# Feed-forward weight pairs by seven products: operand combinations and third weight sums moved to GpSimd, the first pair's first sum to VectorE, the second step as a plain unit

## The reference

```python
def swiglu(x, w_in, w_out):
    gate, up = jnp.split(x @ w_in, 2, axis=-1)      # w_in: 1024 x 5632, w_out: 2816 x 1024
    return (jax.nn.silu(gate) * up) @ w_out

h = layer_norm(DN_ALPHA * h + 0.5 * swiglu(h, ffn_w_in[i, 0], ffn_w_out[i, 0]), ln_g[i, 0], ln_b[i, 0])
```

## Time and profile before

| | us |
|---|---|
| median of 3 runs (1524.52 to 1525.26) | 1524.89 |
| the profiled execution, its own time | 1523.43 |
| its span, first to last instruction | 1521.5 |
| PE busy | 1490.0 (98%) |
| DVE busy | 1112.7 (73%) |
| ACT busy | 833.1 (55%) |
| POOL busy | 156.4 (10%) |
| granted TensorE clock, mean | 0.994 |

### The profile page before, as it was taken

The page is one execution under the profiler, slowest core; times in us unless marked ns, Lnnn a source line. Parts: engine busy times, 40 slices in busy tenths (PEclk is TensorE's granted clock), DMA queues, the critical chain, the costliest instruction groups (busy, mean ns, idle before and its releaser), DMA issues.

```text
span 1521.5 us, 18598 instructions
## 1 busy us (share of the span) xinstructions
PE 1490.0 (98%) x7654; PEld 1258.1 (83%) x7654; DVE 1112.7 (73%) x1135; ACT 833.1 (55%) x839; POOL 156.4 (10%) x152
## 2 busy tenths in 40 slices
PE   8899999989999999999999989999999999999997
PEld 6688888878888788888888868888898888888886
DVE  5887687787877977787567787867686556785555
ACT  5656467565565665554434556555636566354443
POOL 0400020110002000024021200002002200020000
PEclk9999999999999999999999999999999999999999
DMA  9777454477837777555544677746444434465551
GB/s 356 268 231 229 182 204 169 150 262 277 295 106 296 218 241 256 166 227 188 179 160 169 224 249 226 269 163 237 154 167 142 164 139 166 166 222 194 193 191 58
DMA packets 46595, 310.08 MB, mean 204 GB/s; under 512 B 5568, under 2 KB 6016, under 8 KB 10800
## 3 DMA queue, kind: packets, MB, share of 16 engines
q1 hardware_dynamic: 38592, 270.35, 47.8%
q0 software_dynamic: 6112, 34.80, 9.9%
q10 hardware_dynamic: 1808, 3.74, 0.6%
HBM read 282.60 MB, written 1.05 MB: 186 GB/s over the span
## 4 chain that ended last, share of the span: by engine, by line
PE 83%; DVE 7%; DMA 6%; issue 1%; ACT 1%; POOL 1%; SPq 0%; POOLq 0%; DVEq 0%; ACTq 0%
PE psum L1988 16%; PE psum L1992 15%; PE psum L1991 15%; PE psum L2097 7%; PE psum L2124 6%; PE psum L2101 4%; DVE weights_lo L1174 4%; DMA weights_raw_more<-weights_raw_more 3%; PE psum L2240 3%; PE psum L2237 3%; PE psum L2236 3%; PE psum L2131 3%; DMA weights_raw_more<-in_weights 2%; PE psum L2020 1%; PE psum L2033 1%
## 5 line engine op out<-in xcount | busy, mean ns | idle before, releaser
L1174 DVE TENSOR_TENSOR weights_lo<-weights_raw,weights_hi 128x2048 fp32r<-128x2048 f32 x191 | 440.9, 2312 | 198.0 <-ACT weights_hi L609 196.6
L609 ACT ACTIVATE weights_hi<-weights_raw 128x2048 fp32r<-128x2048 f32 (+1 forms) x198 | 372.4, 1883 | 194.9 <-PE psum L1992 136.2
L1174 DVE TENSOR_TENSOR weights_lo<-weights_raw_more,weights_hi 128x2048 fp32r<-128x2048 f32 x56 | 128.2, 2289 | 70.5 <-ACT weights_hi L609 70.5
L1988 PE MATMUL psum<-weights_hi,hidden_hi 128*128 128x512 f32 x416 | 163.9, 394 | 3.3 <-DVE weights_lo L1174 3.3
L1991 PE MATMUL psum<-weights_lo,hidden_hi 128*128 128x512 f32 x416 | 162.4, 390 | 0.0
L1992 PE MATMUL psum<-weights_hi,hidden_lo 128*128 128x512 f32 x416 | 162.1, 390 | 0.0
L1988 PE MATMUL psum<-weights_hi,operand 128*128 128x512 f32 x384 | 151.5, 394 | 0.0
L1991 PE MATMUL psum<-weights_lo,operand 128*128 128x512 f32 x384 | 149.8, 390 | 0.0
L609 ACT ACTIVATE weights_hi<-weights_raw_more 128x2048 fp32r<-128x2048 f32 x56 | 107.1, 1913 | 70.1 <-DMA weights_raw_more<-weights_raw_more 39.2
L1992 PE MATMUL psum<-weights_hi,operand 128*128 128x512 f32 x352 | 137.2, 390 | 0.0
L2097 PE MATMUL psum<-operand,weights_hi 128*128 128x512 f32 x544 | 129.4, 390 | 0.0
(11 more groups left out here) (386 smaller groups left out, 2799.9 us busy)
## 6 DMA issues: line engine op xcount, KB each, us to landing
weights_raw<-in_weights SPq DMA_DIRECT2D x198, 1024.0 KB, 4.8
weights_raw_more<-in_weights SPq DMA_DIRECT2D x56, 1024.0 KB, 8.9
weights_raw_more<-weights_raw_more POOLq DMA_DIRECT2D x20, 1024.0 KB, 7.2
ln_rows<-in_ln_rows POOLq DMA_DIRECT2D x16, 512.0 KB, 7.3
weights_raw_more<-weights_raw POOLq DMA_DIRECT2D x4, 1024.0 KB, 12.3
weights_raw<-in_weights SPq DMA_DIRECT2D x4, 256.0 KB, 4.3
weights_raw<-in_weights SPq DMA_DIRECT2D x2, 512.0 KB, 6.7
normalised<-in_x POOLq DMA_DIRECT2D x2, 512.0 KB, 11.1
```

Source lines behind the costliest of these rows:

```text
L609: nc.scalar.activation(hi[:, rest], whole[:, rest], ACT.Copy).then_inc(hi_split, 1)
L1174: nc.vector.tensor_tensor(lo_of(n), raw_of(n), hi_of(n).bitcast(F32), ALU.subtract).then_inc(lo_split, 1)
L1988: mm(out, a_hi, b_hi, start=start, stop=False, skip_group_check=True)
```

## The change

POOL now makes the four form sums and the four form lo parts (with one more operation, a change of sign, since its forms are add and subtract alone), in the order 0, 3, 2, 1, and t3 of each of the twelve groups. DVE makes t1 of each call's first group, in place of the accumulating DMA; the later t1 and all t4 stay with the DMA. Step 1 is a `features_unit`: its two partial copies on ACT and two sums on DVE are gone, and PE waits, ahead of product b21, for step 1's hidden values (`hid_done`) rather than for the gate sum, since they now lie in the same PSUM banks. The semaphore counts follow.

```diff
+FORM_ORDER, FORM_SUMS = (0, 3, 2, 1), (1, 5, 4, 2)
...
+            def first_forms(f):
+
+                if f:
+                    pool.wait_ge(x_kept, 4 * f)
+                else:
+                    pool.wait_ge(x_lo_done, KC // 2)
+                x11, x12, x21, x22 = x_part(0, 0), x_part(0, 1), x_part(1, 0), x_part(1, 1)
+                nc.gpsimd.tensor_tensor(x22, x22, x21, ALU.subtract).then_inc(form_summed, 1)
+                nc.gpsimd.tensor_tensor(x21, x11, x21, ALU.subtract).then_inc(form_summed, 1)
+                pool.wait_ge(form_summed, 5 * f + 1)
+                nc.gpsimd.tensor_tensor(x11, x22, x11, ALU.add).then_inc(form_summed, 1)
+                pool.wait_ge(form_summed, 5 * f + 3)
+                nc.gpsimd.tensor_tensor(x12, x11, x12, ALU.subtract).then_inc(form_summed, 1)
+                pool.wait_ge(form_summed, 5 * f + 4)
+                nc.gpsimd.tensor_scalar(x11, x11, -1.0, 0.0, ALU.mult, ALU.add).then_inc(form_summed, 1)
+                for at, k in enumerate(FORM_ORDER):
+                    pool.wait_ge(form_hi_done, 4 * f + at + 1)
+                    nc.gpsimd.tensor_tensor(by_chunk(form_lo(k)), in_form[k], by_chunk(form_hi(k)).bitcast(F32),
+                                            ALU.subtract).then_inc(form_ready, 1)
+
+            def add_t3(n0, f, s):
+
+                n = n0 + GROUP_AT[s]
+                t2, t3 = raw_of(n + 1), raw_of(n + 5)
+                pool.wait_ge(lo_split, n + 1)
+                pool.wait_ge(tile_added, tile_sums(f, s) + 1)
+                nc.gpsimd.tensor_tensor(t3, t2, t3, ALU.subtract).then_inc(t3_added, 1)
...
             def add_tiles(n0, f):
 
+                first_forms(f)
                 for s in GROUPS:
                     if s != GROUPS[0]:
                         add_t1(n0, f, s)
+                    add_t3(n0, f, s)
                     add_t4(n0, f, s)
...
-                    split_hi(n + 5, (tile_added, 2 * g + 2))
+                    split_hi(n + 5, (t3_added, g + 1))
...
-                summed_step(1, n0 + 4, 2)
+                act.wait_ge(weights_used, n0 + 4)
+                nc.scalar.activation(silu_g[:, :, :], two(pairs[1][:, 0, :]), ACT.Silu).then_inc(silu_done, 1)
+                split_hi(n0 + 6)
+                act.wait_ge(hid_done, j0 + 2)
+                hidden_hi(j0 + 1, 1, hid[:, 0:2, :])
...
                 split_lo(n0 + 3)
-                form_sums()
                 hidden(j0, pairs[0][:, :, TOK:2 * TOK])
+                add_t1(2)
                 split_lo(n0 + 4)
-                forms_lo()
                 split_lo(n0 + 5)
                 hidden_lo(j0, 0, two(acc[:, 3, :]))
-                summed_step(1, 2)
+                add_t2(2)
+                dve.wait_ge(hid_ready, j0 + 1)
+                hidden(j0 + 1, two(pairs[1][:, 1, :]))
+                split_lo(n0 + 6)
+                hidden_lo(j0 + 1, 1, hid[:, 0:2, :])
...
-                features_both(n0 + 2, unit_banks(1), between=lambda: turn_hidden(j0, 2 * P, acc[:, 3:4, :]), second_free=kept)
+                features_unit(n0 + 2, pairs[1], between={4: turn_first})
...
-                        second_free = lambda: pe.wait_ge(gate_summed, summed_before(f, 2))
+                        second_free = lambda: pe.wait_ge(hid_done, j0 + 2)
```

More of the change, by code:

```diff
@@ L375, in build @@
         group_index = lambda f, s: len(GROUPS) * f + GROUPS.index(s)
+        dma_sums = lambda f, s: (len(GROUPS) - 1) * f + GROUPS.index(s)
+        tile_sums = lambda f, s: (len(GROUPS) + 1) * f + GROUPS.index(s) + 1
         against_hi, against_lo = (lambda t: t[:, :, 0:TOK]), (lambda t: t[:, :, TOK:2 * TOK])
-        summed_before = lambda f, j: SUMMED * f + sum(1 for s in range(1, j) if s not in GROUPS and s - 1 not in GROUPS)
+        summed_before = lambda f, j: SUMMED * f + sum(1 for s in range(2, j) if s not in GROUPS and s - 1 not in GROUPS)
         gate_of = lambda j: pairs[1] if j == 1 else pairs[0]
@@ L533, in _ @@
                 add_t1(N_FFN0, 0, s)
+                add_t3(N_FFN0, 0, s)
                 add_t4(N_FFN0, 0, s)
@@ L685, in forms_hi @@
                 def forms_hi():
-                    for k in range(4):
-                        act.wait_ge(form_summed, 4 * f + k + 1)
+                    for k in FORM_ORDER:
+                        act.wait_ge(form_summed, 5 * f + FORM_SUMS[k])
                         nc.scalar.activation(by_chunk(form_hi(k)), in_form[k], ACT.Copy).then_inc(form_hi_done, 1)
@@ L694, in second_of_next @@
                 def second_of_next(j, n):
-                    split_hi(n, (t1_added, 16 * group_index(f, j) + 16) if j in GROUPS else None)
+                    split_hi(n, None if j not in GROUPS else (t1_added, 16 * dma_sums(f, j)) if j > 2 else (tile_added, tile_sums(f, 2)))
                 def summed_step(j, used, after):
@@ L1313, in last_step @@
                     hidden_lo(j0 + j, j % 3, hid[:, 0:2, :])
[L1315 to L1333, removed]
-                        nc.vector.tensor_tensor(by_chunk(form_lo(k)), in_form[k], by_chunk(form_hi(k)).bitcast(F32),
-                                                ALU.subtract).then_inc(form_ready, 1)
                 def loaded(load):
@@ L1340, in loaded, with add_t1 @@
                     return raw_in(m)
+                def add_t1(s):
+                    b11, b12 = loaded(("up", s, 0)), loaded(("up", s + 1, 0))
+                    nc.vector.tensor_tensor(b12, b12, b11, ALU.add).then_inc(tile_added, 1)
                 def add_t2(s):
@@ L1381, in group @@
                     split_lo(n + 3)
-                    add_t3()
                     split_lo(n + 4)
@@ L2218, in ffn, with turn_first @@
                 unit_banks = lambda j: (gate_of(j), up_of(j))
-                kept = lambda: pe.wait_ge(x_kept, 4 * f) if f else None
-                features_both(n0 + 2, unit_banks(1), between=lambda: turn_hidden(j0, 2 * P, acc[:, 3:4, :]), second_free=kept)
+                def turn_first():
+                    if f:
+                        pe.wait_ge(x_kept, 4 * f)
+                    turn_hidden(j0, 2 * P, acc[:, 3:4, :])
+                features_unit(n0 + 2, pairs[1], between={4: turn_first})
                 def next_down(j, n, hooks={}):
                     pe.wait_ge(hid_ready, j0 + j + 1)
-                    if j == 0:
-                        pe.wait_ge(up_summed, summed_before(f, 2))
+                    if j == 0 and f:
+                        pe.wait_ge(x_kept, 4 * f)
                     at = 2 * (j % 3)
```

18 lines of the change are left out of this document (7 added, 11 removed).

## The result

| | before | after |
|---|---|---|
| median of 5 runs, us | 1524.89 (1523.22 to 1525.26) | 1532.44 (1531.09 to 1532.94) |
| profiled execution, its own time | 1523.43 | 1532.94 |
| its span | 1521.5 | 1530.9 |
| granted TensorE clock, mean | 0.994 | 0.988 |

A forecast was written before the change was run, and what follows sets the result against it. DVE's list behind t1 was taken to bound each call's first group, PE the rest. 1523.4 profiled, +7.2 for first groups, +8.1 for the other eight, +1.5 to the median: 1540 us, range 1516 to 1549.

The forecast's parts named there:

- slower: Whole kernel: the change makes it slower than before, chance 0.71, against 0.06 for the same and 0.23 for faster.
- What bounds: In each call's first group DVE's list behind t1 is the limit; elsewhere it is PE, busy 98% of the span.
- First groups and units, +7.2: First groups of the four calls with their units: third +5.6, fourth +1.3, second +2.3, first -2, together +7.2 us.
- The third call's walk: Third call's first group: PE stalls of 3.1 and 4.5 us around product b21, down tile +5.0 to +6.3, taken +5.6.
- The other eight groups, +8.1: Later groups: t3 on POOL waits until DVE runs dry, 2.7 us lost in three second groups, +8.1 (0 to 10.8).
- rival 2: Second groups: POOL gets its turn behind the running DVE operation, 0.7 us lost in each of four; 1535, chance 0.22.
- Profiled against median, +1.5: Whole kernel: the median of the runs lies 1.5 us above the profiled execution, added to the sum.
- The rule weighed: DVE-POOL shared interface: skill page says issue order decides who blocks; doubted, as POOL, queued first, lost three turns.
- Rival 3: First groups: t3 on POOL doesn't block DVE, falling into its wait; faster, 1514 or down to 1500, chance 0.20.

The follow-up runs named there:

- t1_only: Kernel before with t1 of each first group on DVE in place of the accumulating DMA, nothing else changed: 1506.87 us, ratio 0.9881.
- t3_forms: Kernel after with t3 of all groups and the forms back on DVE, leaving t1 on DVE and the plain unit: 1502.95 us, ratio 0.9857 to before.
- t3_first_dve: Kernel after with t3 back on DVE in the first group of each call alone: 1518.33 us, ratio 0.9959 to before.
- t3_all_dve: Kernel after with t3 of all twelve groups back on DVE: 1517.11 us, ratio 0.9947 to before.
- idle_t3: Kernel with t3 and forms on DVE (1502.95), plus an unused POOL subtraction of 128x2048 in the first groups of calls 1 to 3: 1511.88 us.
- t3_hid_forms: Kernel after with t3 and forms on DVE and the second step's hidden values multiplied ahead of t2: 1504.45 us, ratio 0.9867 to before.

## Why the prediction was right in its sign and wrong in its size

Forecast were 15.1 us more (1540); 7.6 were measured. 1532.44 lies in the range, and slower had 0.71.

- **What bounds.** Right for the kernel before: `t1_only` and `t3_forms` shortened what DVE's list waits for or holds, and the last two calls' first groups came to 19.6 and 18.0. In the kernel after, DVE's list is the limit only up to the split of b21; from there PE's own products, partly at half clock, end the first groups of calls 1 to 3.
- **First groups and units, +7.2.** The sum is right: 5.5 in the groups and 1.4 in the units make 6.9. By call, units with their groups: second +3.1 (forecast 2.3), third +6.4 (5.6), fourth +2.2 (1.3), first -4.8 (-2, 0 to -6). Each later call lies 0.8 or 0.9 above its term, just past the upper end of its bounds, and the first 2.8 below: that the sum fits is in part luck.
- **The third call's walk.** Against b11's start (507.7 forecast, 509.10 measured, of which 1.3 come from calls before): t1's lo part ends 4.4 later forecast, 3.9 measured; t3 on POOL 4.7, 4.57; the split of b21 some 6.5 us, 6.34; PE's stalls 3.1 and 4.5, 2.6 and 3.9 between starts of matmuls; the down tile after 24.3 to 25.7, 25.69. It came to the upper end for the clock, which took an estimated 2.0 us here where the forecast had 1.3:

```profile
517.97:528.20 10.23, 6.96 (x17) 0.50 0.36 74
```

  Half clock was taken for 3.4 us, from the earlier trace rows; here it lasted 10.2 us in the second and third call and 6.8 in the fourth.
- **The other eight groups, +8.1. The step that failed**: 3.1 were measured. The forecast had POOL shut out until DVE paused: t3 "384.9 to 389.6", and 2.7 us lost in each of three second groups. It was drawn from the earlier trace rows, where a residual waited through three DVE instructions. In fact t3 started at 377.36, behind the instruction that DVE was in; the split of b21 took 6.72 and ended at 384.45. PE wants that lo part 7.25 us behind b11's start (5.44 for two products, 1.81 for the hi part of the third), here 385.2: 0.7 spare. Of six second and third groups behind the first call, one lost 0.4. That is rival 2's mechanism. In the first call DVE is 2.4 us later against PE: in its second group t2 is begun 0.66 us ahead of b11, against 3.02 in the second call; and its two groups lost 1.8 and 0.9. In `t3_first_dve` t2 is begun 3.4 us ahead in that group, t3 is on POOL as well, and it takes 16.3. Between the medians of `t3_first_dve` and `t3_all_dve` the eight are worth 1.2.
- **Profiled against median, +1.5.** Before, the profiled execution lay 1.5 below the median; after, 0.5 above. The terms say 10.0 for spans that differ by 9.4; the medians differ by 7.6. These 2 us are no more than the spread of the five runs, 2.0 before and 1.9 after. Of the 7.5 us by which the forecast was too high, 5.0 are the term of the eight groups, and 2.0 are this one.
- **The rule weighed.** POOL, ready first, got the turn behind the DVE instruction that ran, in all twelve groups. By that the Trainium skill, page "SBUF — State Buffer", section "Who interferes with whom", was the better guide than the earlier trace rows: who issues first has the port. The trace agrees for every t3; it doesn't for the residual of 39.49 in `t3_forms`, which waited.
- **Rivals.** Rival 3 (t3 doesn't block) is refuted by the split of 6.34 us in the kernel after, and by `idle_t3`. Rival 2, 1535, was the nearest: it was right on the turn. That its 2.8 us come near the 3.1 is luck: it had 0.7 in the second group of each call, and the losses lie in the first call's two groups and one third group. The stated range begins at 1516, though most of rival 3's chance was put at 1514.
- **Not seen.** The forecast treated the parts as one. They are opposite: t1 on DVE -18.2, the unit -3.9 beside it, the forms on POOL and t3 on POOL +29.5 together (14.5 and 15.3 alone). That makes +7.4, the result.

## What to carry to other kernels

Before work is moved to POOL to relieve DVE, look at what DVE does at that time: where both read two SBUF tiles they took turns here, and 2.2 us taken off DVE's list came back as 4.1 to 4.4 of standing, for the instruction that is next, wanted or not. In these runs the move did no harm only where DVE had that much slack ahead of what PE wants, and there it gained nothing either. A stall of PE can cost more than its own length: an estimated 2.0 us of half clock came on top of 1.9 us of DVE's list. Try the parts of a change one by one: here one part was worth 18 us and two others hid it.

## What the runs showed of the hardware that was not expected

- POOL's subtraction of 128x2048 took 4.57 us with two different input tiles (t3) and 3.60 with the same tile as both inputs, and DVE's stand shrank with it, 4.06 to 3.10.
- The turn goes to POOL at the next boundary between DVE instructions, in all t3 of all runs that had one. The first call's residual is the exception, in four kernels: in the one before it lost three boundaries and got in at the fourth, and in `t1_only`, `t3_forms` and `idle_t3` it waited until a DVE instruction read PSUM, 10 us on. In the kernel after and in the others where it wasn't held back it got in at the next boundary; in `t3_hid_forms` that was after the same DMA issue on POOL and as far into the same DVE split (0.83 us) as in `t3_forms`. What makes the difference is open; it wasn't tried by itself.
- In the third call of the kernel after, the granted clock fell to half at 517.97, 1.0 us after a stall of 2.3 us, and stayed there for 10.2 us, through a second stall of 3.3 (PE's work began again at 516.98 and 523.25). In `t3_all_dve`, with one stall of 2.28 us there, it stayed full; in the second call, behind one of 2.62, it was halved for 3.4 us. In `t3_forms`, whose longest wait in a first group is 1.8 us between starts, it was full until the last 7 us.
